# A two-layer decoder trunk on one core: the state-space scan's side work in other slots, and its copies and multiplier on ScalarE

## What is computed

```python
xr = jnp.einsum('blgh,gph->blgp', uf, bbr)
xi = jnp.einsum('blgh,gph->blgp', uf, bbi)
a_r = jnp.broadcast_to(ar, (1, seq, S5_GROUPS, S5_STATE))
a_i = jnp.broadcast_to(ai, (1, seq, S5_GROUPS, S5_STATE))
_, _, hr, hi = lax.associative_scan(_complex_linear_combine, (a_r, a_i, xr, xi), axis=1)
y = (jnp.einsum('blgp,ghp->blgh', hr, c_re.astype(f32))
     - jnp.einsum('blgp,ghp->blgh', hi, c_im.astype(f32)))
y = y.reshape(bsz, seq, S5_WIDTH) + d.astype(f32) * u.astype(f32)
...
proj = h @ e_w_in[j]
u, z_s5, q, k, v, z_da = jnp.split(proj, e_splits, axis=-1)
```

## Time and profile before

| | us |
|---|---|
| median of 3 runs (952.48 to 952.61) | 952.5 |
| the profiled execution's own time | 952.75 |
| its span, from the first to the last instruction | 951.0 |
| PE busy | 936.0 (98%) |
| DVE busy | 610.0 (64%) |
| ACT busy | 575.4 (60%) |
| POOL busy | 111.3 (12%) |

### The profile page before, as it was taken

How to read it: one execution, slowest core, us unless ns; L and a number is a source line. 1 busy time by engine, 2 the same in 40 slices (tenths; PEclk the granted TensorE clock), 3 DMA queues, 4 the chain that set the end, 5 groups by cost and what they waited for, 6 DMA issues and landing times.

```text
span 951.0 us, 15769 instructions
## 1 busy us (share of the span) xinstructions
PE 936.0 (98%) x5939; PEld 796.3 (84%) x5939; DVE 610.0 (64%) x971; ACT 575.4 (60%) x928; POOL 111.3 (12%) x126
## 2 busy tenths in 40 slices
PE   7999999999999999999999999999999999999998
PEld 7998888778878999888888788888888888888886
DVE  4688889799797954855644555555555555555553
ACT  4689886876967746544545573555456545554332
POOL 3101002011020000000002540220021002200000
PEclk9999999999999999999999999999999999999999
DMA  8776544445343467555999986668999866654662
GB/s 285 185 190 196 156 133 134 136 135 175 112 140 127 137 198 266 179 192 190 175 166 180 195 239 169 182 174 160 171 160 172 197 175 178 176 175 156 212 213 85
DMA packets 116007, 165.83 MB, mean 174 GB/s; under 512 B 19301, under 2 KB 56298, under 8 KB 115690
## 3 DMA queue, kind: packets, MB, share of 16 engines
q1 hardware_dynamic: 99504, 159.67, 64.0%
q10 hardware_dynamic: 16442, 5.33, 2.3%
HBM read 162.86 MB, written 2.11 MB: 173 GB/s over the span
## 4 chain that ended last, share of the span: by engine, by line
PE 82%; ACT 7%; DVE 6%; issue 3%; DMA 1%; POOL 1%; ACTq 0%; SPq 0%; DVEq 0%
PE bank L456 21%; PE bank L458 21%; PE bank L457 21%; PE bank L483 3%; PE bank L484 3%; PE bank L485 3%; ACT wh L969 2%; ACT res L1078 2%; PE bank L600 1%; ACT res L1090 1%; DVE wl L977 1%; ACT scr L1230 1%; DVE scr L1747 1%; PE bank L592 1%; DMA res<-in_x 1%
## 5 line engine op out<-in xcount | busy, mean ns | idle before, releaser
L977 DVE TENSOR_TENSOR wl<-raw,wh 128x1024 fp32r<-128x1024 f32 x295 | 362.0, 1231 | 252.7 <-ACT wh L969 251.5
L969 ACT ACTIVATE wh<-raw 128x1024 fp32r<-128x1024 f32 x295 | 310.5, 1058 | 190.2 <-PE bank L458 119.5
L456 PE MATMUL bank<-wh,xh 128*128 128x512 f32 x768 | 307.1, 400 | 0.3 <-DVE wl L977 0.3
L458 PE MATMUL bank<-wh,xl 128*128 128x512 f32 x768 | 300.0, 391 | 0.0
L457 PE MATMUL bank<-wl,xh 128*128 128x512 f32 x768 | 299.2, 390 | 0.0
L458 PEld LDWEIGHTS bank<-wh,xl 128*128 128x128 f32 x768 | 144.1, 188 | 31.1
L456 PEld LDWEIGHTS bank<-wh,xh 128*128 128x128 f32 x768 | 144.3, 188 | 29.0 <-DVE wl L977 0.7
L457 PEld LDWEIGHTS bank<-wl,xh 128*128 128x128 f32 x768 | 144.5, 188 | 27.7
L456 PE MATMUL bank<-wh,yh 128*128 128x512 f32 x256 | 100.5, 393 | 0.0
L458 PE MATMUL bank<-wh,yl 128*128 128x512 f32 x256 | 99.7, 390 | 0.0
L457 PE MATMUL bank<-wl,yh 128*128 128x512 f32 x256 | 99.6, 389 | 0.0
(11 more groups left out here) (317 smaller groups left out, 1022.4 us busy)
## 6 DMA issues: line engine op xcount, KB each, us to landing
raw<-in_o_w_in SPq DMA_DIRECT2D x128, 512.0 KB
raw<-in_e_w_in SPq DMA_DIRECT2D x130, 256.0 KB, 3.3
raw<-in_e_w_out SPq DMA_DIRECT2D x32, 512.0 KB
raw<-in_o_w_out SPq DMA_DIRECT2D x32, 512.0 KB
raw<-in_e_w_in SPq DMA_DIRECT2D x31, 512.0 KB
raw<-in_s_w_glu SPq DMA_DIRECT2D x8, 512.0 KB
res<-in_x SPq DMA_DIRECT2D x8, 256.0 KB, 6.8
res<-in_x SPq DMA_DIRECT2D x1, 2048.0 KB, 9.6
```

The source lines that it names most:

```text
L456: nc.tensor.matmul(o, l_hi, w_hi, start=first, stop=False)
L458: mm = nc.tensor.matmul(o, l_lo, w_hi, start=False, stop=last)
L969: nc.scalar.activation(wh[:, j % RING, :], raw[:, j % RING, :], ACT.Copy).then_inc(hi_done, 1)
L977: nc.vector.tensor_tensor(wl[:, j % RING, :], raw[:, j % RING, :], wh[:, j % RING, :].bitcast(F32), ALU.subtract).then_inc(lo_done, 1)
```

## The change

- `s5_powers`' first part goes from slot 6 to slot 8 (`BA_SLOT`), `s5_far`'s second part from slot 12 to slot 11 (`FAR_SLOT`).
- The two parts of `angles` go from slot 0 to slots 14 and 15 of the step ahead (`TAB_SLOT`); `table`, always one slot behind the second part, thereby goes from slot 1 to slot 0.
- B's and C's power 0 are no longer computed by products with 1 but copied on ScalarE (new `s5_own`, slot 10); `s5_powers` takes powers 1 to 4 in place of 0 to 3, `s5_far` powers 1 to 3 in place of 0 to 4, so its three instructions for each part have 384 elements a partition in place of 640. `s5_pad` copies four powers in place of five.
- `s5_hold` goes from VectorE (one instruction) to ScalarE (8 instructions of 64 elements a partition), in slot 13 as before.
- `s5_low` of batches 0, 1 and 2 goes from slot 15 of steps 1, 2 and 3 to slots 10, 11 and 13 of the fifth stretch (`LOW_SLOT`).

```diff
-TAB_SLOT, FAR_SLOT, BA_SLOT = [0, 0], [-7, -4], [-10, -4]
+TAB_SLOT, FAR_SLOT, BA_SLOT = [-2, -1], [-7, -5], [-8, -4]
...
+LOW_SLOT = {10: 0, 11: 1, 13: 2, 15: 3}
...
                 if h == 0:
                     pe.wait_ge(cc_done, 2 * i + 2)
+                    pe.wait_ge(b0_done, i + 1)
...
+            def s5_own(i):
+
+                if i:
+                    act.wait_ge(y_ps, i)
+                    act.wait_ge(near_ps, 2 * i)
...
+                for r in range(2):
+                    nc.scalar.activation(cc[r][:, :, 0, :], bc_all[:, i, 2 + r, :].rearrange("p (i h) -> p i h", h=16), ACT.Copy)
+                for g in range(2):
+                    at = slice(64 * g, 64 * g + 64)
+                    ins = nc.scalar.activation(b0[at, :, :, 16 * g:16 * g + 16],
+                                               bc_all[at, i, 0:2, :].rearrange("p r (i h) -> p r i h", h=16), ACT.Copy)
+                ins.then_inc(b0_done, 1)
+
+            def s5_hold(i):
+
+                act.wait_ge(h_done, 2 * i) if i else act.wait_ge(prm_exp, 3)
+                for t in range(TB):
+                    ins = nc.scalar.activation(mg[:, t, :], later, ACT.Copy, scale=mag_all[:, TB * i + t:TB * i + t + 1])
+                ins.then_inc(hold_done, 1)
+
             def s5_pad(i, r):
 
+                act.wait_ge(b0_done, i + 1)
                 act.wait_ge(cc_done, 2 * i + (r + 1))
...
                     at = s5_at(n, s, i)
                     if TAB_SLOT[1] + 1 == at:
                         table(i)
+                    if OWN_SLOT == at:
+                        s5_own(i)
+                    if HOLD_SLOT == at:
+                        s5_hold(i)
...
-                    x = bc_all[:, i, 2 + f, :].rearrange("p (i k h) -> p i k h", k=1, h=16).to_broadcast([P, TB, 5, 16])
-                    y = pw[:, k, :, a_].rearrange("p k (i h) -> p i k h", h=1).to_broadcast([P, TB, 5, 16])
+                    x = bc_all[:, i, 2 + f, :].rearrange("p (i k h) -> p i k h", k=1, h=16).to_broadcast([P, TB, HOP - 1, 16])
+                    y = pw[:, k, 1:HOP, a_].rearrange("p k (i h) -> p i k h", h=1).to_broadcast([P, TB, HOP - 1, 16])
...
-            def s5_hold(i):
-                x = mag_all[:, TB * i:TB * i + TB].rearrange("p (i c) -> p i c", c=1).to_broadcast([P, TB, NCH])
...
                 if h == 0:
                     dve.wait_ge(near_ps, 2 * i + 2)
                     dve.wait_ge(ca_done, i + 1)
+                    dve.wait_ge(hold_done, i + 1)
...
-                    if HIGH_SLOT + 1 == at:
-                        s5_low(i)
+                if n == DA_PAIRS and s in LOW_SLOT:
+                    s5_low(LOW_SLOT[s])
```

More of the change, by code:

```diff
@@ L67 @@
 FOX_LINKS, FOX_POOL_LINKS = 12, 4
-TAB_SLOT, FAR_SLOT, BA_SLOT = [0, 0], [-7, -4], [-10, -4]
+TAB_SLOT, FAR_SLOT, BA_SLOT = [-2, -1], [-7, -5], [-8, -4]
 T_SLOT = [-2, -1, -1, -1]
-NEAR_SLOT, HOLD_SLOT, SKIP_SLOT = [-1, 2], -3, -8
+NEAR_SLOT, HOLD_SLOT, SKIP_SLOT, OWN_SLOT = [-1, 2], -3, -8, -6
 X_SLOT, YN_SLOT, Y_SLOT = [0, 3], 7, [8, 8]
@@ L262, in build @@
         bt = [flat[:, 4096 + 512 * k:4608 + 512 * k].rearrange("p (a h) -> p a h", a=GP) for k in range(2)]
-        ca_t, *cc = [flat[:, at:at + 640].rearrange("p (i k h) -> p i k h", i=TB, k=5) for at in (3072, 3840, 4480)]
+        ca_t = flat[:, 3072:3456].rearrange("p (i k h) -> p i k h", i=TB, k=HOP - 1)
+        cc = [flat[:, at:at + 512].rearrange("p (i k h) -> p i k h", i=TB, k=HOP) for at in (3840, 4480)]
         ba_t = [x.rearrange("p r n -> p (r n)").rearrange("p (i s h) -> p i s h", i=TB, s=HOP) for x in prod]
@@ L276, in build @@
         keep = res.rearrange("p t n -> p (t n)")
-        ca = keep[:, 0:2560].rearrange("p (r i k h) -> p r i (k h)", r=2, i=TB, k=5)
-        near = keep[:, 2560:3584].rearrange("p (i n) -> p i n", i=TB)
+        ca = keep[:, 0:2048].rearrange("p (r i k h) -> p r i (k h)", r=2, i=TB, k=HOP)
+        near = keep[:, 2048:3072].rearrange("p (i n) -> p i n", i=TB)
+        b0 = keep[:, 3072:3584].rearrange("p (r i h) -> p r i h", r=2, i=TB)
         pw = keep[:, 3584:3904].rearrange("p (r k i) -> p r k i", r=2, k=5)
@@ L315, in build @@
             ("t_ps", "xin_sb", "near_ps", "near_sb", "x_ps", "x_read", "h_done", "y_ps"))
+        b0_done, hold_done = sem("b0_done"), sem("hold_done")
         gelu_done, s5_hi, s5_lo, v_out = sem("gelu_done"), sem("s5_hi"), sem("s5_lo"), sem("v_out")
@@ L678, in s5_near @@
                     for r in range(2):
-                        nc.tensor.matmul(o[0:32, at:at + 64], ba[:, r, t, 0:32],
-                                         cc[r][:, t, 0:HOP, :].rearrange("p k h -> p (k h)"), start=r == 0, stop=False)
+                        nc.tensor.matmul(o[0:32, at:at + 64], b0[:, r, t, :],
+                                         cc[r][:, t, :, :].rearrange("p k h -> p (k h)"), start=r == 0, stop=False)
                     mm = nc.tensor.matmul(o[0:32, at:at + 16], ident[:, 32 * e:32 * e + 32],
@@ L721, in s5_out_y @@
                         for e in range(TH):
-                            mm = nc.tensor.matmul(tokens_at(h, k, e, 1), ca[:, r, TH * h + e, 32 * (k + 1):32 * (k + 2)],
+                            mm = nc.tensor.matmul(tokens_at(h, k, e, 1), ca[:, r, TH * h + e, 32 * k:32 * k + 32],
                                                   hst[h][:, r, e * NCH:(e + 1) * NCH - 1], start=False, stop=r == 1,
@@ L1080, in s5_near @@
                 ins.then_inc(near_sb, 1)
+            def s5_own(i):
+                if i:
+                    act.wait_ge(y_ps, i)
+                    act.wait_ge(near_ps, 2 * i)
+                else:
+                    act.wait_ge(zeros, 2)
+                    act.wait_ge(bc_b, 1)
+                    act.wait_ge(bc_c, 4)
+                for r in range(2):
[10 more added lines that the diff above has]
+                ins.then_inc(hold_done, 1)
             def s5_pad(i, r):
+                act.wait_ge(b0_done, i + 1)
                 act.wait_ge(cc_done, 2 * i + (r + 1))
@@ L1088, in s5_pad @@
                     at = slice(64 * g, 64 * g + 64)
-                    dst = ca[at, r, :, :].rearrange("p i (k h) -> p (i k) h", k=5)[:, :, 16 * g:16 * g + 16]
+                    dst = ca[at, r, :, :].rearrange("p i (k h) -> p (i k) h", k=HOP)[:, :, 16 * g:16 * g + 16]
                     ins = nc.scalar.activation(dst, cc[r][at].rearrange("p i k h -> p (i k) h"), ACT.Copy)
@@ L1591, in powers @@
                 pr, pi = pw[:, 0, :, :], pw[:, 1, :, :]
-                v.memset(pr[:, 0, :], 1.0)
-                v.memset(pi[:, 0, :], 0.0)
                 for k in (1, 2):
@@ L1668, in times @@
                 def times(o, f, k):
-                    x = bc_all[:, i, 2 + f, :].rearrange("p (i k h) -> p i k h", k=1, h=16).to_broadcast([P, TB, 5, 16])
-                    y = pw[:, k, :, a_].rearrange("p k (i h) -> p i k h", h=1).to_broadcast([P, TB, 5, 16])
+                    x = bc_all[:, i, 2 + f, :].rearrange("p (i k h) -> p i k h", k=1, h=16).to_broadcast([P, TB, HOP - 1, 16])
+                    y = pw[:, k, 1:HOP, a_].rearrange("p k (i h) -> p i k h", h=1).to_broadcast([P, TB, HOP - 1, 16])
                     return v.tensor_tensor(o, x, y, ALU.mult)
-                times(cc[r], r, 0)
+                o = cc[r][:, :, 1:HOP, :]
+                times(o, r, 0)
                 link(times(ca_t, 1 - r, 1))
-                flat_of = "p i k h -> p (i k h)"
-                v.tensor_tensor(cc[r].rearrange(flat_of), cc[r].rearrange(flat_of), ca_t.rearrange(flat_of),
+                v.tensor_tensor(*(x.rearrange("p i k h -> p i (k h)") for x in (o, o, ca_t)),
                                 ALU.subtract if r else ALU.add).then_inc(cc_done, 1)
                 dve.wait_ge(cc_done, 2 * i + (r + 1))
-            def s5_hold(i):
-                x = mag_all[:, TB * i:TB * i + TB].rearrange("p (i c) -> p i c", c=1).to_broadcast([P, TB, NCH])
-                y = later.rearrange("p (i c) -> p i c", i=1).to_broadcast([P, TB, NCH])
-                link(v.tensor_tensor(mg[:, :, :], x, y, ALU.mult))
             def s5_powers(i, r):
@@ L1690, in times @@
                     x = bc_all[:, i, f, :].rearrange("p (i s h) -> p i s h", s=1, h=16).to_broadcast([P, TB, HOP, 16])
-                    y = pw[:, k, 0:HOP, a_].rearrange("p s (i h) -> p i s h", h=1).to_broadcast([P, TB, HOP, 16])
+                    y = pw[:, k, 1:HOP + 1, a_].rearrange("p s (i h) -> p i s h", h=1).to_broadcast([P, TB, HOP, 16])
                     return v.tensor_tensor(o, x, y, ALU.mult)
@@ L1772, in s5 @@
                         s5_skip(i)
-                    if at == HOLD_SLOT:
-                        s5_hold(i)
                     for h in range(2):
```

## The result

| | runs | median us | lowest to highest us |
|---|---|---|---|
| before | 4 | 952.49 | 950.87 to 952.61 |
| changed | 4 | 968.1 | 966.43 to 972.02 |

The medians are 15.6 us apart, 1.6%. The ratio of the changed kernel to the one before, taken from the means, is 1.0174, with a 95% interval of 1.0138 to 1.021: the change costs time, clear of the noise. The forecast was 963 us, in a stated range of 954.5 to 970 us. The profiled execution of the changed kernel took 966.43 us, with a span of 964.7 us, against 952.75 us and 951.0 us before.

A forecast was written before the change was run, and what follows sets the result against it. TensorE, busy 98% of the span, was taken as the bound, VectorE's list as without slack. Periods of 17.1 + 38.0 + 3.2 + 5.7 = 64.0 us put the last mark 10.6 us later: 963 us, range 954.5 to 970 us.

The forecast's parts named there:

- The step that decided: `table` in slot 0, 3.18 us with its table load, delays ScalarE's copy of part 1, which TensorE's transposes await.
- The waits at the transposes of part 3: Sign of being right: TensorE waits 2 to 5 us there, four times, put down to ScalarE's copy.
- the mark: End of `s5_near(0)` on ScalarE, start of slot 0's split; forecast 64.0 us apart, against 60.54 and 61.51 before.
- VectorE's list from slot 5 to the end of `angles`: VectorE's stretch without slack: 36.70 - 1.58 - 0.68 - 0.68 + 4.27 = 38.0 us.
- From the end of `table` to the mark: Copies, transposes, `s5_pad(0)` and `s5_near(0)` in chain: 5.7 us.
- First mark: First batch, where `table` has no load: forecast at 118.0 us, 2.1 us late.
- drain: The skill page's price beside a function-table load, about 1.4 us; the prediction said the trace doesn't agree.
- `s5_hold` on ScalarE: Eight small activations in slot 13: between 1.3 and 2.7 us, 2 taken, costed at nothing in the sum.
- Rival C: TensorE's clock falls to 1.2 GHz after three pauses, 2 to 4 us more each: 969 to 975 us, chance 0.10.
- signs of being wrong: Marks 60 to 61 us apart, VectorE idle between slots 5 and 15, or a slice with lower granted clock.
- the waits at L564: TensorE's three waits for `head_out`, 2.7 us, forecast to go with `s5_powers`' first part moved to slot 8.
- up to 4 us a step: Cost of ScalarE's `s5_hold` and `s5_own` without the cover of idle time and its 2.8 us wait for `angles`.

The follow-up runs named there:

- e3_table_late: Changed kernel with `table` alone one slot later, in slot 1 behind the copies, `angles` staying in slots 14 and 15: 949.67 us, ratio 0.9972.
- e1_tab_back: Changed kernel with `TAB_SLOT` back at [0, 0], so `angles` in slot 0 and `table` in slot 1: 950.28 us, ratio 0.9977.
- e8_low_back: e5_fill with the three early `s5_low` parts back in slot 15: 964.71 us, ratio 1.0133.
- e2_tab_alone: Kernel before with one edit, `TAB_SLOT` at [-2, -1], so `angles` in slots 14 and 15 and `table` in slot 0: 979.54 us, ratio 1.0292.
- e5_fill: Changed kernel with 14 unread matmuls on TensorE ahead of part 3's transposes in the three batches with 3.9 us pauses: 963.24 us, ratio 1.0112.
- e6_ba_alone: Kernel before with one edit, the first part of `s5_powers` in slot 8: 951.61 us, ratio 0.9999.
- e4_load_ahead: Changed kernel with one more single-column Sin ahead of `table`'s wait for `angles`, loading the function table early: 960.15 us, ratio 1.0086.

## Why the prediction was right, and where it was short

**The direction and the mechanism.** The step that decided, `table` ahead of the copies with VectorE's list behind it, held link by link. The waits at the transposes of part 3 came four times, put down to ScalarE's copies, 1.97 and three times 3.9 us long, against 2 to 5 us forecast. ScalarE waited 2.98 us ahead of `table` (2.8 forecast), and the second part of `angles` began 54.2 us behind the mark (235.61 - 181.37; 53 forecast). e3_table_late takes back the place of `table` alone, e1_tab_back that of `angles` as well, and both bring the whole loss back. That VectorE's list is the other half is shown by e8_low_back and e2_tab_alone, where 0.68 and 2.94 us more in the list lengthen each period by 0.64 and 2.9 us.

**The terms.** VectorE's list from slot 5 to the end of `angles`: 38.0 us forecast, 38.0 measured. `table`: 3.2 and 3.18. From the end of `table` to the mark: 5.7 forecast; 6.63 us at the second batch, where the clock was down already (174.74 to 181.37), 5.70 us at the third (241.17 to 246.87), and 5.7 us in e5_fill at the second (178.05 to 183.74). First mark: 2.1 us late forecast; it came 0.45 us late, but this execution was 1.5 us ahead by then (the copy of part 0 started at 104.16 us, before at 105.64 us), so it is 1.9 us late against its own start. The activation behind the load of 1.28 us starts 1.29 us after the load does (172.21 to 173.50 us), so no drain beside it shows here either. `s5_hold` on ScalarE: 2 us taken, and 2.00 us measured; `s5_own` 0.7 to 1.5 us bounded:

```profile
217.40 0.53 ACT L1097 ACTIVATE scr<-early 128x128 f32<-128x128 f32 x2
217.80 0.84 ACT L1100 ACTIVATE res<-early 64x256 f32<-64x256 f32 x2
...
225.71 2.00 ACT L1108 ACTIVATE mg<-con,scr 128x64 f32<-128x64 f32 x8
```

These are, in the order of the lines, the copies of C's and B's power 0 (1.24 us from 217.40 us to the end) and the eight instructions of the multiplier.

**What it was short of.** Rival C, the fall of the clock, had a chance of 0.10 beside my forecast, as if one excluded the other, and a lower granted clock stood among the signs of being wrong. Both happened. The term that I left out of the sum is the clock's: the period is 64.1 us with it up and 65.0 to 65.5 us with it down. That is why 968.1 us lies 0.6 us above the forecast's own range (959 to 967.5 us) and inside the stated one, whose upper part stood there for the near half of C. The size of the term by the profiled execution: the span is 13.7 us longer, and all of TensorE's waits together are 8.3 us longer. (Those at L670 are 13.7 us; against them stand 2.7 at L564, 1.0 at L679, 0.7 at `s5_in_x`, and 1.0 in the wait for the first load of x, 2.3 us before and 1.3 us here, an input's arrival and no effect of the change.) The remaining 5.4 us are slower matmuls, as TensorE's busy time also has it, 5.5 us more. By e5_fill they are 4.9 us. I had priced the fall at 2 to 4 us for each of three pauses; it was about 1.8 us each, a little under the lower end. Where the lost time stands differs from batch to batch: at the second, 0.9 us is in the copies' chain; at the third that chain has its 5.70 us again, but ahead of it TensorE was late in slots 1 to 4, and VectorE began slot 5 at 18.58 us behind the mark (181.37 to 199.95), where it was 17.14 us in e5_fill (183.74 to 200.88) and 17.1 us forecast.

**What stands only in the experiments.** The prediction counted the waits at L564 as won, 2.7 us. Where the loss is taken away, part of that comes back as the next late item: in e1_tab_back and e3_table_late the norm of slot 11, which `s5_far`'s move to slot 11 made late, and in e6_ba_alone the second `head_out`. My sentence that moving `s5_far` "changes no sum up to slot 12" was true of the sum, and overlooked who waits in the middle of it. And "up to 4 us a step" for ScalarE's new work without cover was too much: in e1_tab_back it has no wait for `angles` to hide in, and costs nothing that can be seen.

## What to carry to other kernels

An item that is moved earlier takes its waits with it: ask what its engine would have done next, and whether that is what the bounding engine waits for. Here `table` took on the lateness of a list without slack (VectorE's) and stood at the head of the path that the bounding engine waits for (ScalarE's copies); one slot later, it was harmless. Where the engine that bounds the kernel is made to pause, add the clock to the wait; filling the pause with idle matmuls shows how much of the loss is the clock's.

## What was not expected of the hardware

TensorE's clock fell behind pauses as short as 1.97 us, but not behind each: after the first batch's pause of 1.97 us it fell to 0.50 in e5_fill (0.54 over 113 to 116 us) and in e8_low_back, and stayed at 1.00 in the changed kernel and in e4_load_ahead; after three pauses of 2.5 us in e4_load_ahead it fell twice, and one stretch stayed at 1.00. Behind all three pauses of 3.9 us in the changed kernel it fell to 0.50, for 3.4 to 6.8 us. In the kernel before, from 13 us on, pauses of up to 1.23 us left it up. The Trainium skill ("TensorE: Matmul & The Clock Gate", HAM oscillation) says that pauses bring back the lower level, which these rows bear out, at shorter pauses than I had expected. The changed kernel's four runs spread over 5.6 us, while e4_load_ahead's four lie within 1.4 us and e5_fill's within 2.7 us. Falls that come or don't explain at most a part of it: the mean granted clock is 0.993 in the runs of 966.43 and 969.58 us and 0.991 in those of 966.62 and 972.02 us, so runs of equal clock lie 3 and 5 us apart. What the rest is stays open.
